# Time mixes of a four-layer network: triangular blocks of 32 instead of 16 inverted on VectorE, and the order of the recurrence rewritten

## The reference, cut to what matters

```python
def step(state, inp):
    r_t, w_t, k_t, v_t, kk_t, a_t = inp
    sa = jnp.einsum('bhvk,bhk->bhv', state, -kk_t)
    state = (state * w_t[:, :, None, :]
             + sa[..., None] * (kk_t * a_t)[:, :, None, :]
             + v_t[..., None] * k_t[:, :, None, :])
    return state, jnp.einsum('bhvk,bhk->bhv', state, r_t)
```

## Time and profile before

| | |
|---|---|
| median of 3 runs | 2975.98 us (2972.99 to 2976.99) |
| the profiled execution | 2970.36 us, its span 2968.7 us |
| granted clock of TensorE, mean | 0.989 |
| TensorE busy | 2887.0 us (97%) |
| VectorE busy | 2289.3 us (77%) |
| ScalarE busy | 1404.7 us (47%) |
| DMA, mean | 206 GB/s |

### The profile page before, as it was taken

One profiled execution on the slowest core, in us unless ns is written; L12 is line 12 of the kernel. 1 busy time (PEld: TensorE's weight loads), 2 busy tenths in 40 slices (PEclk: granted clock), 3 DMA queues, 4 the chain that ended last, 5 costly groups with the idle time before them and its releaser, 6 DMA issues. The chain is left out here.

```text
span 2968.7 us, 49895 instructions
## 1 busy us (share of the span) xinstructions
PE 2887.0 (97%) x20006; PEld 2559.8 (86%) x20006; DVE 2289.3 (77%) x3308; ACT 1404.7 (47%) x2292; POOL 97.2 (3%) x187
## 2 busy tenths in 40 slices
PE   7999999999999999999999999999999999999998
PEld 6887898888889888888886888887888888989887
DVE  6987678898878857888877888886555867775785
ACT  4544224545555734545544555544323544565553
POOL 0000000000000000000000000000000000000000
PEclk9999999999999999999999999999999999999999
DMA  8784527685665337676764667672403553443453
GB/s 346 256 317 172 199 89 269 245 335 214 250 239 213 125 115 270 227 263 255 261 242 169 236 241 262 243 284 105 168 12 128 192 192 129 171 160 145 181 186 131
DMA packets 74168, 611.27 MB, mean 206 GB/s; under 512 B 11952, under 2 KB 12128, under 8 KB 36320
## 3 DMA queue, kind: packets, MB, share of 16 engines
q1 hardware_dynamic: 42768, 459.36, 41.5%
q0 software_dynamic: 26352, 144.59, 13.0%
q10 hardware_dynamic: 4832, 4.24, 0.5%
HBM read 605.02 MB, written 3.15 MB: 205 GB/s over the span
## 5 line engine op out<-in xcount | busy, mean ns | idle before, releaser
L1076 ACT ACTIVATE unit_high<-weights 128x1024 fp32r<-128x1024 f32 x576 | 609.8, 1060 | 621.0 <-PE psum L1145 332.2
L1087 DVE TENSOR_TENSOR unit_low<-weights,unit_high 128x1024 fp32r<-128x1024 f32 x576 | 703.5, 1223 | 145.0 <-ACT unit_high L1076 144.7
L1141 PE MATMUL psum<-h_part,unit_high 128*128 128x512 f32 x3024 | 767.9, 393 | 3.7 <-DVE h_part L998 3.7
L1141 PEld LDWEIGHTS psum<-h_part,unit_high 128*128 128x128 f32 x3024 | 541.4, 189 | 103.4 <-DVE h_part L998 5.0
L1145 PEld LDWEIGHTS psum<-h_part,unit_low 128*128 128x128 f32 x3024 | 416.2, 190 | 30.8
L1145 PE MATMUL psum<-h_part,unit_low 128*128 128x256 f32 x3024 | 431.8, 282 | 0.0
L333 PE MATMUL psum<-in_part,w_part 128*128 128x256 f32 x2784 | 360.1, 290 | 16.9 <-issue 6.9
L333 PEld LDWEIGHTS psum<-in_part,w_part 128*128 128x128 f32 x2784 | 346.8, 195 | 25.8 <-issue 17.9
L1162 PE MATMUL psum<-hidden,unit_high 128*128 128x512 f32 x1386 | 348.3, 392 | 0.0
L524 DVE SCALAR_TENSOR_TENSOR ada_sum<-ada_in,c_act,ada_sum 128x1536 f32<-128x1536 f32 x154 | 278.7, 1813 | 31.3 <-DMA ada_in<-in_ada_w 31.2
L1282 DVE TENSOR_REDUCE arena<-psum 128x256 f32<-128x512 f32 x378 | 260.4, 689 | 48.4 <-PE psum L1145 37.9
(11 more groups left out here) (335 smaller groups left out, 2760.6 us busy)
## 6 DMA issues: line engine op xcount, KB each, us to landing
weights<-in_weights SPq DMA_DIRECT2D x290, 1536.0 KB, 6.6
ada_in<-in_ada_w POOLq DMA_DIRECT2D x182, 768.0 KB, 5.9
consts<-in_consts POOLq DMA_DIRECT2D x1, 1414.0 KB, 13.1
x<-in_x SPq DMA_DIRECT2D x1, 1024.0 KB, 9.1
v_first<-arena ACTq DMA_DIRECT2D x1, 1024.0 KB, 6.6
arena<-v_first ACTq DMA_DIRECT2D x1, 1024.0 KB, 4.7
weights<-in_weights SPq DMA_DIRECT2D x1, 512.0 KB, 5.5
near_rows<-arena ACTq DMA_DIRECT2D x2, 256.0 KB, 7.0
```

What stands on the lines that cost most here:

```text
L1076: k.nc.scalar.activation(k.unit_part[0][:, n % UNIT_RING], w, ACT.Copy).then_inc(k.sem["unit_high"], 1)
L1087: k.nc.vector.tensor_tensor(k.unit_part[1][:, n % UNIT_RING], w, k.unit_part[0][:, n % UNIT_RING].bitcast(FP32), ALU.subtract).then_inc(k. ...
L1141: mm(k.psum[:, 2 * (j % 2) + half, :].rearrange("p (i t) -> p i t", i=2), lhsT=part(2 * j + half, 0, t), rhs=k.h_parts[:, :, t], start=t = ...
```

## The change

Blocks of 32 x 32 are inverted, one in each of 128 partitions, by a chain of 31 steps of two instructions. `choose` goes, with the constants that it used; ScalarE's copy now writes straight into the tile that is sent. The way out to HBM is cut into two transfers for two units each, in runs of 32 floats (128 bytes) where it had 64 floats (256 bytes); the last step back is cut too, unit 0 first. `base_out` stands behind the seventh of the eight tiles of v, and `base_in` behind the last. `level16`, `x32` and `y32` are gone from TensorE and VectorE. The order of the passes is changed on both engines: on TensorE `rest` comes first, then `level32`, `first_outs`, `upper`, `turn_out`, `receptances`, `across`, `y64`, `lower`, and `state_and_out` and `near_again` stand between the two halves of `keys`; on VectorE `open_y` and `turn_y` of the next unit stand ahead of `keys`, and so do one or two of the sums, while others come behind `centre`. Before the loop `open_y` and `turn_y` of unit 0 stand behind `ended`.

```diff
-        self.low = k.raw_flat[0:64, 0:1024].rearrange("p (s u t) -> p u s t", s=16, u=UNITS)
-        self.inverse = k.raw_flat[0:64, 1024:2048].rearrange("p (s u t) -> p u s t", s=16, u=UNITS)
+        self.step = k.small[:, 192:448]
+        self.near_t = cut(26, 1024).rearrange("p (u m t) -> p u m t", u=UNITS, m=8)
+        self.low = k.raw_flat[:, 0:1024].rearrange("p (s t) -> p s t", s=32)
+        self.inverse = k.raw_flat[:, 1024:2048].rearrange("p (s t) -> p s t", s=32)
...
+        self.base = k.raw_flat[:, 0:1024].rearrange("p (u m t) -> p u m t", u=UNITS, m=8)
...
-    def level16(c):
+    def level32(c):
         at("wk_am", c)
         at("wk_x_read", c)
         half_products(c, 0, 0, half_of_near(c), z.x[c.hf], s["wk_lx"])
 
-    def x32(c):
-        at("wk_t", c, 0, 2)
-        half_products(c, 0, 1, half_of(z.y[c.hf]), z.t[c.hf], s["wk_x32"])
-
-    def y32(c):
+    def receptances(c):
         if c.b:
             pe.wait_ge(s["wk_out_read"], UNITS * j + c.u - 1)
-        half_products(c, 1, 0, half_of(z.t[c.hf]), z.y[c.hf], s["wk_y32"])
-
-    def level32(c):
-        at("wk_x32_read", c)
-        half_products(c, 0, 0, half_of_near(c), z.x[c.hf], s["wk_lx"])
-
-    def receptances(c):
...
-    level16(head)
     turn_values(0)
     turn_values(1)
-    x32(head)
-    y32(head)
     level32(head)
     turn_ended(0)
+    receptances(head)
     y64(head)
-    receptances(head)
     keys(head, lambda: turn_ended(1))
     pe.wait_ge(s["rw_turned_read"], 2 * (j + 1))
     near_again(units[1])
     for n in range(1, UNITS):
         head, tail = units[n], units[n - 1]
-        if n == 1:
-            rest(tail)
-        level16(head)
         with_mod = n == UNITS - 1 and j == 0
         if with_mod:
             at("wk_rk_read", tail, 0, 2)
             mod_sums(k, pe, pr, 2, range(6))
-        if n > 1:
-            rest(tail)
+        rest(tail)
+        level32(head)
         if with_mod:
             pe.wait_ge(s["mod_rows_read"], 3)
         first_outs(tail)
...
         if n >= 2:
             turn_out(units[n - 2])
-        x32(head)
-        across(tail)
         if with_mod:
             pe.wait_ge(s["mod_ready"], 3)
-        y32(head)
+        receptances(head)
+        across(tail)
+        y64(head)
         lower(tail)
-        level32(head)
-        state_and_out(tail)
-        y64(head)
-        receptances(head)
-        if n + 1 < UNITS:
-            pe.wait_ge(s["wk_sa_read"], 2 * (UNITS * j + n))
-            near_again(units[n + 1])
-        else:
-            early_outputs(0)
-        keys(head)
+
+        def between():
+            state_and_out(tail)
+            if n + 1 < UNITS:
+                pe.wait_ge(s["wk_sa_read"], 2 * (UNITS * j + n))
+                near_again(units[n + 1])
+            else:
+                early_outputs(0)
+
+        keys(head, between)
     tail = units[3]
     early_outputs(1)
...
-            ins = act_(z.near_q[u % 2][part].rearrange("p (i n) c -> p i n c", i=2), ps[:, :, :, part], f.Copy)
+            ins = act_(z.near_t[part, u].rearrange("p (i n) c -> p i n c", i=2), ps[:, :, :, part], f.Copy)
...
-        act.wait_ge(s["near_moved"], 64 * j + 16 * step)
-
-    def low_out():
-        act.wait_ge(s["near_chosen"], UNITS * (j + 1))
-        act.dma_start(by_row, z.near_t.rearrange("p m u t -> p m (u t)")).then_inc(s["near_moved"], 16)
+        act.wait_ge(s["near_moved"], 80 * j + 16 * step)
+
+    def low_out(b):
+        act.wait_ge(s["wk_near_read"], UNITS * j + 2 * b + 2)
+        act.dma_start(by_row[:, 16 * b:16 * b + 16], z.near_t[:, 2 * b:2 * b + 2].rearrange("p u m t -> p (u m) t"))\
+            .then_inc(s["near_moved"], 16)
 
     def low_in():
-        moved(1)
-        act.dma_start(k.raw_flat[0:64, 0:1024], by_block).then_inc(s["near_moved"], 16)
+        moved(2)
+        act.dma_start(k.raw_flat[:, 0:1024], by_block).then_inc(s["near_moved"], 16)
 
     def base_out():
         act.wait_ge(s["wk_base"], j + 1)
-        act.dma_start(by_block, k.raw_flat[0:64, 1024:2048]).then_inc(s["near_moved"], 16)
+        act.dma_start(by_block, k.raw_flat[:, 1024:2048]).then_inc(s["near_moved"], 16)
 
     def base_in():
-        moved(3)
-        act.dma_start(k.wkv_base[:, :].rearrange("p (m x) -> p m x", m=8), by_row).then_inc(s["near_moved"], 16)
+        moved(4)
+        for first, end, signal in ((0, 1, "near_moved"), (1, UNITS, "base_moved")):
+            act.dma_start(z.base[:, first:end].rearrange("p u m t -> p (u m) t"), by_row[:, 8 * first:8 * end])\
+                .then_inc(s[signal], 16)
...
         evacuate("r", m, z.r[:, m], f.Copy)
         if m == 3:
+            low_out(0)
             near_read(2)
             near_read(3)
         if m == 4:
-            low_out()
+            low_out(1)
         if m == 5:
             low_in()
     act.wait_ge(s["rw_keys"], 3 * j + 1)
     for m in range(KT):
         evacuate("v", m, z.v[:, m], f.Copy)
-        if m == 2:
+        if m == 6:
             base_out()
-        if m == 3:
-            base_in()
+    base_in()
...
-        dve.wait_ge(s["near_moved"], 64 * j + 32)
+        dve.wait_ge(s["near_moved"], 80 * j + 48)
         x, low = z.inverse, z.low
-        for c in range(15):
-            n, w = c + 1, 15 - c
-            step = z.step[:, 0:UNITS * n * w].rearrange("p (u r c) -> p u r c", u=UNITS, r=n)
-            own.of(v.tensor_tensor(step, low[:, :, c, n:16].unsqueeze(2).to_broadcast([64, UNITS, n, w]),
-                                   x[:, :, 0:n, c:n].to_broadcast([64, UNITS, n, w]), mult))
-            own.of(v.tensor_tensor(x[:, :, 0:n, n:16], x[:, :, 0:n, n:16], step, sub))
+        for c in range(31):
+            n, w = c + 1, 31 - c
+            step = z.step[:, 0:n * w].rearrange("p (r c) -> p r c", r=n)
+            own.of(v.tensor_tensor(step, low[:, c, n:32].unsqueeze(1).to_broadcast([P, n, w]),
+                                   x[:, 0:n, c:n].to_broadcast([P, n, w]), mult))
+            own.of(v.tensor_tensor(x[:, 0:n, n:32], x[:, 0:n, n:32], step, sub))
...
-    choose(0)
-    choose(1)
     value_mixes()
-    choose(2)
-    choose(3)
     open_inverse()
     beside()
     invert()
...
     def open_y(c):
         if c.b:
             dve.wait_ge(s["wk_sa"], 2 * (UNITS * j + c.u - 1))
-        dve.wait_ge(s["near_moved"], 64 * (j + 1))
-        same = k.const("same16_half").rearrange("p (c t) -> p c t", t=16).unsqueeze(1).to_broadcast([P, 4, 4, 16])
+        if c.u:
+            dve.wait_ge(s["base_moved"], 16 * (j + 1))
+        else:
+            dve.wait_ge(s["near_moved"], 80 * (j + 1))
...
     chunks = [RwUnit(k, j, u) for u in range(UNITS)]
     head = chunks[0]
     projected("g1", 1)
-    open_y(head)
-    turn_y(head)
     if j:
         mixed_values(0)
         mixed_values(1)
     ended()
+    open_y(head)
+    turn_y(head)
     values(0)
     values(1)
-    level16(head)
+    level32(head)
+    receptances(head)
+    y64(head)
+    open_y(chunks[1])
+    turn_y(chunks[1])
     beside()
-    x32(head)
-    y32(head)
-    level32(head)
-    open_y(chunks[1])
-    y64(head)
-    turn_y(chunks[1])
-    receptances(head)
     keys(head, 0)
     keys(head, 1)
     for n in range(1, UNITS):
         head, tail = chunks[n], chunks[n - 1]
         if n == UNITS - 1 and j == 0:
             mod_rows(k, dve, 2)
-        level16(head)
+        level32(head)
         if n >= 2:
             variance(chunks[n - 2])
-            beside()
             normed(chunks[n - 2])
-        else:
-            beside()
         if n == UNITS - 1 and j == 0:
             mod_columns(k, dve, own, 2)
-        x32(head)
+        receptances(head)
         across(tail)
-        y32(head)
-        if n == 2:
-            beside()
-        level32(head)
+        y64(head)
+        if n + 1 < UNITS:
+            open_y(chunks[n + 1])
+            turn_y(chunks[n + 1])
+        beside()
         if n >= 2:
             gated(chunks[n - 2])
         else:
             beside()
-        if n + 1 < UNITS:
-            open_y(chunks[n + 1])
-        beside()
-        y64(head)
-        if n + 1 < UNITS:
-            turn_y(chunks[n + 1])
-        receptances(head)
         keys(head, 0)
         keys(head, 1)
         centre(tail)
+        beside()
+        if n == 2:
+            beside()
```

More of the change, by code:

```diff
@@ L220, in const_parts @@
         "head_ones": same,
-        "halves16": row[:, 0:1] // 16 % 2 == np.arange(2)[None, :],
-        "same_row": row % 16 == np.arange(16)[None, :],
         "causal_before": np.concatenate([row <= col, row < col], 1),
     }
-    for b in (4, 5):
-        s = 1 << b
-        h = np.arange(64)[None, :]
-        low = (r // (2 * s) == h // (2 * s)) & (r // s % 2 == 1) & (h // s % 2 == 0)
-        parts[f"level{b}"] = -1.0 * low
-    parts["same16_half"] = r // 16 == np.arange(64)[None, :] // 16
+    h = np.arange(64)[None, :]
+    parts["level5"] = -1.0 * ((r // 32 % 2 == 1) & (h // 32 % 2 == 0))
+    parts["same32_half"] = r // 32 == h // 32
```

(33 more changed lines are left out.)

25 lines of the change are left out of this document (11 added, 14 removed).

## The result

The changed kernel takes 3014.57 us (median of four runs, 3009.92 to 3022.21), the kernel before 2976.32 on the same chip (2972.99 to 2976.99): a ratio of 1.0141, 95% interval 1.0126 to 1.0157 (the two medians alone give 1.0129). The forecast was 2988.3, the range 2979 to 3000. The sign was right; 26 us were missing. The profiled execution took 3013.0, its span is 3011.3, 42.6 us over that of before.

A forecast was written before the change was run, and what follows sets the result against it. TensorE and VectorE were both taken as nearly full in the first mix. First mix +10.1 us, second -1.4 and clock +3.6 gave +12.3: 2982.7 for the profiled execution, 2988.3 for the median, range 2979 to 3000.

The forecast's parts named there:

- Work removed: TensorE's passes: level16, x32 and y32 go, 2.0 us per pass to gain; pass 1 of the second mix 2.7 shorter.
- Inversion: VectorE's chain in each mix: 22.9 us, 11.6 more, from 316.4 to 339.4, covered by 1.3 us only.
- The third rival: Small-row transfers land 3 to 5 us later, the inversion leaves its cover: +16 to +20, 2992 to 2996; chance 0.15.
- Head: Stretch before each mix's first rest: 1.8 us later in the first mix, 0.9 in the second.
- Passes of the first mix: Pass 1 +0.3 us, pass 2 +1.9, the sixteenth sum +5.4, pass 3 -0.3.
- the two waits: TensorE idle in the first mix: over 4 us at the end of pass 1, some 9 before mod_sums.
- my 10.1: The first mix's forecast loss in us, from its start to its end, without any loss to the clock.
- Clock: Half-speed TensorE after two long waits in the first mix: 0 to 3 us each, 1.8 taken, +3.6 in all.
- The wait of the earlier trace: Kernel before: 4.07 us without a matmul, then granted clock 0.50 over 5.7 us; the forecast's basis for pricing low clock.
- the products' gain comes through: TensorE last in every pass, so six passes gain 2.0 us each, less 2.7 for the heads: -9.3, 2967; chance 0.08.
- It cancels out: Clock stays up, the wait for the sums costs 2 us, the head nothing: +3.5, 2979.5; chance 0.12.
- the low end: Whole kernel: the forecast with no clock loss and half of the head and of the sums, 2988 - 9 = 2979.

The follow-up runs named there:

- Run 1: The changed kernel with extra dense products of a constant put into TensorE's waits ahead of passes 2 and 3 of both mixes: 2986.72 us, ratio 1.005.
- runs 6 and 7: Changed kernel with v_first's load earlier and the old pass order, 2959.55 us; then that with receptances behind lower and further moves, 2956.24, repeated 2961.88.
- the second of run 4: Changed kernel with VectorE's sums and gated ahead of turn_y, late sums behind normed, and TensorE's receptances behind across, y64 and lower: 2985.83 us, ratio 1.0053.
- run 2: Kernel before, with only sums 15 and 16 of the first mix moved behind centring: 2985.65 us; the same with 20 dense products ahead of mod_sums: 2977.39.
- run 5: The changed kernel with the second mix's load of v_first issued ahead of the way back of the inverses: 3013.65 us, ratio 1.0133.

## Why the prediction was right in sign and wrong in size

- **Work removed**: held. TensorE's work in pass 1 of the second mix is 16.22 us for 19.68, the pass is 2.5 us shorter for a forecast 2.7.
- **Inversion**: 314.51 to 337.86 is 23.35 us for 22.9, and it started 1.9 earlier than I took. The last transfer out did land later, after 8.1 us (7.6 in the second mix) for the 7.0 of before, but it was issued 1.1 us earlier (303.09 for 304.21), since no `choose` stands ahead of it; the transfer in took 3.3 for 3.4 although its bytes had doubled. On the way back 384 KB took 4.7 us in the first mix and 9.2 in the second, where in before 256 KB had taken 2.9 in either. The rule of the Trainium skill that I set beside it (DMA: Bandwidth & Descriptors, Specifications), that such rows fall off line rate, agrees with the trace in direction only: 1.1 and 0.6 us more for the same bytes, with rows of 128 bytes for 256, and both are under its 512. The third rival, which needed 3 to 5 us there, fell. The gate mixes began at 337.93 and were in time.
- **Head**: +1.8 was too much, -0.5 came. The base went out and back sooner than I walked it: its way in was issued at 342.4, not 346, and ScalarE read g2 at 352.43 for a forecast 353.9.
- **Passes of the first mix**: the two waits are there, each with its cause. Pass 1 came to 21.2 us for 20.8, with a wait of 4.74; the end of the keys in pass 2, most of which ran at half clock, at 30.8 us behind rest for 22.5; receptances waited 1.59 for ScalarE for a forecast 1.7; mod_sums waited 9.37 for "some 9", and started 5.09 us behind the end of the keys for 5.16 (1.5 + 3.46 + 0.2). Run 1, which has the waits nearly without the low clock, gives +10.1 for my 10.1.
- **Clock, the step that failed**: "For each 0 to 3 (half of the 5.5); I take 1.8: +3.6". I read its price off, where 24 dense matmuls of 256 columns follow the wait and the clock is back after 5.7 us, and carried that to passes of thin products, as 1.8 us for each of two waits. Here it stayed at half for 20.5 and 41.0 us, and for 23.9 (2242.2 to 2266.1) in pass 3 of the second mix. Run 1 puts the price at 23 to 28 us in all. The wait of that third place, 2.61 us, I hadn't even priced; the second mix, forecast 1.4 us shorter, came out 11.5 longer from the last rest of the first, 9.6 of it in that pass. The wait of the earlier trace rows isn't the longest of the trace, though its heading says so: there is one of 12.07 us at the start. And there is one of 3.03 us (up to 234.44), behind which the clock was 0.50 until 239.0: a wait of that size had a price before the change. The nearest row by size of wait was not the nearest by what follows it. That it is the thinness that keeps the clock down is read from such pairs of rows; no run changed what follows a wait and left the wait. The Trainium skill (TensorE: Matmul & The Clock Gate, Why this matters for your kernels) names the direction, that gaps send the clock back to half; how long it stays there with such products was mine to ask.
- **A term left out**: v_first in the second mix. I wrote that base_in is issued and what stands behind it on ScalarE's queue, but not the load of v_first behind it on the DMA queue: 11.0 us to land for 4.7 before, with open_y and turn_y +4.2 us at the first rest for the +0.9 forecast. About 2 of the 4.2 are again the clock, which was at half behind the 4.61 us wait: turn_values took 3.6 us for 2.2 and level32 1.6 for 1.1.
- **Rivals**: "the products' gain comes through" was decided where I said, at the masked keys. It did not come here; with level32 put back ahead of rest it came, in runs 6 and 7. "It cancels out" needed the clock to stay up, and it did not.
- **Slips in the forecast's sums**: no clock loss and half of the head and of the sums are 3.6 + 0.9 + 2.7 = 7.2, not 9, so the low end is 2981; and 3 to 5 us on top of 12.3 are +15 to +17, not +16 to +20. Neither would have brought 3014.57 into the range.

What stays open: what exactly lets the clock fall. A wait of 0.65 us stood ahead of a pass mostly at half clock in one profile and ahead of the same pass at full clock in another; one of 1.39 us stood ahead of either within one profile (the second of run 4). That the wait ahead of TensorE's thin products matters is shown by runs 1 and 2; a limit is not.

## What to carry to other kernels

Price a new wait of TensorE by what it does behind it: dense products had the clock back after 5.7 us, a chain of thin ones mostly ran at half clock for 17 to 41 us, which costs some 10 us a pass, at times for waits of 3 us and less. When work is taken from TensorE, keep a piece of it that needs nothing (here level32 of the next unit) in the place where it used to cover another engine's step; with the same products one order is 38 us over the kernel before and another, with v_first moved as well, 12 under it. And when a step's transfers are split or moved, look at what stands behind them on the same DMA queue, not only on the issuing engine.

## What the runs showed that I had not expected

- Low clock lasting through a busy engine: 281 matmul records, busy 33.73 of 41.00 us (5.6 of the rest being the wait), at a granted clock of 0.50, and 228 records busy 29.93 of 29.93 us at a mean of 0.60.
- The same code in two executions: a pass of 20.36 us and one of 29.93.
- Adding work made the kernel faster by 23 to 28 us (run 1) and by 8 (run 2).
- 1 MB behind the 512 KB in rows of 128 bytes on one queue took 13.8 and 11.0 us to land, where it took 6.6 and 4.7; issued ahead of them it took 4.9 (run 5), and they then 9.4 and 11.2 for 2.7 and 9.2. The issue of that load alone took 4.57 us on ScalarE's queue behind the small rows (0.33 ahead of them).
